# Feed-forward up product of pairs 2 to 21: seven quarter products of 256 columns in place of eight

## The chip, the cores and the metric

The kernel runs on one core of a Trainium2 chip. The metric is the device time of one execution in microseconds (us), lower is better. A core has five engines that matter here: PE (TensorE, the matrix engine, with PEld for its weight loads), DVE (VectorE), ACT (ScalarE), POOL (GpSimd) and SP, which issues most of the DMAs. They run side by side and wait for one another through semaphores.

## The reference, cut to what matters

The reference is two transformer blocks for 512 tokens of width 1024. The change is in the feed-forward part of the first block:

```python
h = _rmsnorm(x, g_pre_ffn[i])                       # 512 tokens x 1024
u = _causal_dwconv(h @ w_up[i], w_conv[i], b_conv[i])  # w_up: 1024 x 5632
a, v = u[..., :D_FF], u[..., D_FF:]                 # D_FF = 2816, 22 tiles of 128
x = x + _rmsnorm((jax.nn.gelu(a) * v) @ w_down[i], g_post_ffn[i])
```

All of it is float32. The product `h @ w_up` is the up product; its first 2816 columns are the gate, the others the value.

## The kernel before, in words

**The precision.** A float32 product is made of three products of rounded parts. Each operand is split into a high part (the value rounded to fp32r) and a low part (the rest), and high x high, high x low and low x high are added up in PSUM. The names ending in `_r` are such fp32r views.

**The tiling.** Weights come from HBM as tiles of 128 x 1024 f32 (512 KB), the list `W`, into the 12 slots of `ring`. The up product has 44 tiles from number `W_UP` on: tile 2j holds the weights of gate features 128j to 128j+127, tile 2j+1 those of the value. A **pair** is such a couple, j = 0 to 21 (`NF` = 22). A tile is eight blocks of 128 x 128, one for each eighth (k) of the width 1024.

**One tile on each engine.** ACT makes the high part (`high_act`, L379: `ring` to `arena_r`, 1024 columns), POOL the low part (`low_pool`, L394: tile minus high), PE runs `split_features`: 16 matmuls of 512 columns with the high weights (L431, tokens high and low in turn) and 8 with the low weights (L434). Split tiles have two places, so the high part of tile t+2 is made when tile t has been used. The tokens are `hT_r` (high) and `up_low`, 128 x 512 for each k.

**Behind the product.** Each tile leaves 128 features x 512 tokens in one of eight PSUM banks. The causal convolution of width 3 along the tokens is three operations: ACT scales and adds the bias from PSUM (`conv_last`, L2763), DVE adds the two shifted taps (L3065 and L3067, scalar_tensor_tensor with `u` in PSUM, the view `banks`, and the sum `c` in SBUF, the view `arena`). When both tiles of a pair are done ACT takes the gelu of the gate (L2770) and DVE multiplies the two (L3071) into `gT`, the rows of the down product that follows.

**The order.** Every engine runs a list written out by hand. PE's list has the 44 tiles one after the other, pair by pair, with one wait on `up_dve` four pairs back. ACT's has, for each tile, the high part of the tile two ahead and then `conv_last`. POOL's has one low part after another. DVE's has four tap operations and one multiplication for each pair. SP loads tile n into its slot when the tile 12 before it has been used. Rows 0 and 1 of the down product's tokens are split by DVE in the last pair, the others behind it, by `split_dve` (L420 the high part, L421 the low).

## Time and profile before

| | before |
|---|---|
| device time, median of 3 runs | 1540.62 us (1538.61 to 1542.84) |
| profiled execution, its own time | 1538.59 us |
| its span (first to last instruction) | 1536.8 us |
| granted TensorE clock, mean | 0.995 |
| PE busy | 1495.9 us, 97% of the span |
| DVE, ACT, POOL busy | 667.6, 508.5, 513.6 us |

The profile is of one execution. Its own time is 1.8 us more than its span and 2.0 us less than the median. An engine's busy time is the union of its instructions; matmuls are pipelined, so the start of one to the start of the next tells what one costs, not its duration. The two letters behind a name tell the direction: `banks<-hT_r,arena_r` writes PSUM from two tensors of SBUF. A name in SBUF is anything but `banks`.

### The profile page before, as it was taken

Reading aid. Unit: us, or ns where it says so; the run is one execution under the profiler, and the core shown is the slowest. Engines: PE = TensorE matmul, PEld = TensorE weight load, DVE = VectorE, ACT = ScalarE, POOL = GpSimd, SP = SyncE. Lnnn points to the kernel's source line nnn. Section 1 sums busy time; section 2 is a strip of 40 time slices with the busy share of each in tenths; the row PEclk is TensorE's granted clock in tenths of the full one; section 3 lists DMA queues with packets and bytes.
Section 4 is the critical chain, followed back from the end, with each engine's and each line's share of the span. In section 5 each row is a group of like instructions: output and inputs, shape, how many; then the busy total and the mean of one; then the engine's idle time right before and its main releaser. Section 6 shows DMA issues by size and latency. Waiting matters only on the chain.

```text
span 1536.8 us, 19531 instructions
## 1 busy us (share of the span) xinstructions
PE 1495.9 (97%) x7629; PEld 1019.5 (66%) x7630; DVE 667.6 (43%) x1141; ACT 508.5 (33%) x917; POOL 513.6 (33%) x328
## 2 busy tenths in 40 slices
PE   8999999999999999999999999999999999999997
PEld 7976677888788888888888777468543443433433
DVE  4157664224733333423335778664533232332334
ACT  4246664223533333321246333424111111111112
POOL 3454664445344444444724362622100010010000
PEclk9999999999999999999999999999999999999999
DMA  8233002322322222232323222267999999999996
GB/s 313 98 109 95 1 2 97 98 100 99 115 96 96 96 96 96 97 97 99 97 92 122 91 82 69 109 256 289 361 429 428 431 418 430 429 429 421 424 426 252
DMA packets 52636, 306.87 MB, mean 200 GB/s; under 512 B 7098, under 2 KB 7354, under 8 KB 40001
## 3 DMA queue, kind: packets, MB, share of 16 engines
q1 hardware_dynamic: 47872, 292.03, 49.2%
q0 software_dynamic: 4096, 11.49, 2.0%
q10 hardware_dynamic: 576, 2.10, 0.3%
q8 instruction: 63, 1.03, 0.3%
q14 instruction: 29, 0.23, 0.1%
HBM read 303.39 MB, written 4.19 MB: 200 GB/s over the span
## 4 chain that ended last, share of the span: by engine, by line
PE 86%; DMA 6%; DVE 5%; ACT 1%; POOL 1%; issue 1%; SPq 0%; DVEq 0%; ACTq 0%
PE banks L431 19%; PE banks L1256 13%; PE banks L476 12%; PE banks L434 9%; DMA ring<-experts 6%; PE banks L1302 5%; PE banks L1311 3%; PE banks L1056 2%; PE banks L456 2%; PE banks L2484 2%; PE banks L2468 2%; PE banks L2550 1%; PE banks L2454 1%; PE banks L914 1%; PE banks L915 1%; PE banks L2443 1%
## 5 line engine op out<-in xcount | busy, mean ns | idle before, releaser
L394 POOL TENSOR_TENSOR arena_r<-ring,arena_r 128x1024 fp32r<-128x1024 f32 x143 | 353.2, 2475 | 414.1 <-ACT arena_r L379 394.5
L379 ACT ACTIVATE arena_r<-ring 128x1024 fp32r<-128x1024 f32 x143 | 150.5, 1058 | 441.4 <-PE banks L434 279.4
L431 PE MATMUL banks<-hT_r,arena_r 128*128 128x512 f32 x640 | 250.0, 391 | 0.0
L431 PE MATMUL banks<-arena_r 128*128 128x512 f32 x640 | 249.1, 389 | 0.0
L1256 PE MATMUL banks<-ring,arena 128*64 128x512 f32 x704 | 222.5, 605 | 12.0 <-DMA ring<-experts 12.0
L476 PE MATMUL banks<-arena_r 128*128 128x512 f32 x784 | 183.5, 389 | 0.6 <-DVE arena_r L421 0.6
L476 PEld LDWEIGHTS banks<-arena_r 128*128 128x128 f32 x784 | 147.1, 188 | 31.5 <-POOL arena_r L394 1.0
L1256 PEld LDWEIGHTS banks<-ring,arena 128*64 128x64 f32 x704 | 70.5, 139 | 142.4 <-issue 141.5
L431 PEld LDWEIGHTS banks<-hT_r,arena_r 128*128 128x128 f32 x640 | 120.1, 188 | 29.0 <-issue 3.4
L431 PEld LDWEIGHTS banks<-arena_r 128*128 128x128 f32 x640 | 120.2, 188 | 25.1 <-issue 0.2
L751 POOL MEMSET arena<- 128x1024 f32 x15 | 14.3, 952 | 341.8 <-PE banks L1209 332.8
L434 PE MATMUL banks<-hT_r,arena_r 128*128 128x512 f32 x520 | 128.4, 389 | 0.0
L1949 DVE TENSOR_TENSOR resid<-resid,banks 128x1024 f32<-128x1024 f32 x60 | 70.6, 1218 | 127.2 <-PE banks L1311 127.2
L1302 PE MATMUL banks<-arena 128*64 128x512 f32 x496 | 113.6, 595 | 2.5 <-DMA arena<-experts 2.2
L1256 PE MATMUL banks<-arena 128*64 128x512 f32 x278 | 115.9, 595 | 0.0
L434 PEld LDWEIGHTS banks<-hT_r,arena_r 128*128 128x128 f32 x520 | 97.6, 188 | 20.3
L3065 DVE SCALAR_TENSOR_TENSOR arena<-banks,colt,arena 128x511 f32<-128x511 f32 x44 | 33.0, 750 | 151.8 <-ACT arena L2763 151.8
L1302 PEld LDWEIGHTS banks<-arena 128*64 128x64 f32 x496 | 36.5, 137 | 66.3 <-issue 60.5
L1311 PE MATMUL banks<-arena_r,colt_r 128*128 128x512 f32 x256 | 67.5, 404 | 0.1
L1518 ACT ACTIVATE arena<-banks 128x512 f32<-128x512 f32 x16 | 9.6, 597 | 165.6 <-PE banks L1268 165.6
L1311 PEld LDWEIGHTS banks<-arena_r,colt_r 128*128 128x128 f32 x256 | 45.5, 188 | 23.4 <-issue 14.6
L1938 DVE SCALAR_TENSOR_TENSOR arena_r<-banks,colt,arena_r 128x512 fp32r<-128x512 f32 x32 | 24.0, 751 | 82.2 <-ACT arena_r L1548 82.2
(506 smaller groups left out, 2171.6 us busy)
## 6 DMA issues: line engine op xcount, KB each, us to landing
ring<-stream SPq DMA_DIRECT2D x164, 512.0 KB, 3.3
arena<-experts SPq DMA_DIRECT2D x35, 2048.0 KB, 15.6
ring<-experts SPq DMA_DIRECT2D x32, 2048.0 KB, 16.6
ring<-experts SPq DMA_DIRECT2D x17, 1024.0 KB, 17.3
arena<-experts SPq DMA_DIRECT2D x31, 512.0 KB, 10.1
arena<-experts SPq DMA_DIRECT2D x11, 1024.0 KB, 15.9
ring<-experts SPq DMA_DIRECT2D x14, 512.0 KB, 6.4
hT<-experts SPq DMA_DIRECT2D x8, 512.0 KB, 11.0
```

What stands on the lines that cost most here:

```text
L379: nc.scalar.activation(parts(name, m)[:, 0, :], tile(tile_n), ACT.Copy).then_inc(S["w_high"], 1)
L394: nc.gpsimd.tensor_tensor(w[:, 1, :], tile(tile_n), plain(w[:, 0, :]), ALU.subtract).then_inc(S["w_low"], 1)
L431: nc.tensor.matmul(pb[:, bank, :], w[:, 0, k * P:(k + 1) * P], b[:, k, :], start=(k == 0 and part == 0), stop=False)
L434: last = nc.tensor.matmul(pb[:, bank, :], w[:, 1, k * P:(k + 1) * P], high[:, k, :], start=False, stop=(k == ND - 1))
L456: last = nc.tensor.matmul(pb[:, bank0 + i, 0:width], a[:, k, i * P:(i + 1) * P], w[:, v, q * width:(q + 1) * width], start=(k == 0 and par ...
L476: last = nc.tensor.matmul(pb[:, 2 * i + h, :], u[row], w[:, v, h * 512:(h + 1) * 512], start=(k == 0 and row + v == 0), stop=(k == K - 1 a ...
L1056: last = nc.tensor.matmul(pb[:, 2 * i + h, :], rows[row][:, i * P:(i + 1) * P], w[:, v, h * 512:(h + 1) * 512], start=(k == 0 and part == ...
L1256: last = nc.tensor.matmul(pb[r, bank, :], XT[:, k, r], weights(b, c + e, k * 512, (k + 1) * 512), start=(k == 0), stop=(k == ND - 1))
L1302: last = nc.tensor.matmul(pb[r, 3 + h, :], hbT[:, k, r], weights(b, 4 + e, at, at + 512), start=(k == 0), stop=(k == 3))
L1311: last = nc.tensor.matmul(pb[:, bank, :], spread_r[:, i * P:(i + 1) * P], y[:, h * 512:(h + 1) * 512], start=(part == 0), stop=(part == 1 ...
L1949: TT(half, half, pb[:, first:second + 1:second - first, :], ALU.add).then_inc(S["added"], 1)
L3065: L(nc.vector.scalar_tensor_tensor(out=c[:, 1:T], in0=u[:, 0:T - 1], scalar=col("w_conv", 2 * NF + m), in1=c[:, 1:T], op0=ALU.mult, op1=AL ...
```

## The change

Pairs 0 and 1 (`PLAIN_PAIRS` = 2) stay as they are. In each of the twenty pairs 2 to 21 (`MIXED`) the two tiles are seen as a 2 x 2 array of quarters: gate or value, by the first or the second half of the width (`gate_1`, `gate_2`, `value_1`, `value_2`, each 128 x 512). The tokens are a 2 x 2 array too: first or second half of the width by the first or last 256 tokens (`x_1` to `x_4`). The product of two 2 x 2 arrays takes eight quarter products; here seven are made (Strassen's scheme in Winograd's form), of sums of weight quarters (`s1` to `s4`) with sums of token quarters (`t1` to `t4`), and the four output quarters are put together from them.

- **PE** runs `up_term` seven times a pair: 8 matmuls of 256 columns with the high part of the term's weights, 4 with the low part.
- **DVE** makes the token sums once (8 operations over 128 x 1024, and four low parts of the same size). For each pair it makes the four weight sums (`weight_sums`, 128 x 512 each) and seven joins (`join`, 128 x 256, a quarter product in PSUM added to something in SBUF), the last of which leave gate and value as rows in `junk`, which is SBUF. The four taps now read `junk` instead of PSUM.
- **ACT** makes seven high parts of 128 x 512 for a pair (`term_high`) in place of two of 128 x 1024, and a copy of the first quarter product (`take_first`).
- **POOL** makes seven low parts of 128 x 512 in place of two of 128 x 1024.
- Each of the seven terms has one place for its split weights, so the high part of term q of pair j+1 waits for PE to be done with term q of pair j. The tiles of these pairs use 6 slots of the ring, the other six hold the parts of `t1`, `t2` and `t4`. Several semaphores are merged under new names (`mg_sig` and `pg_sig` to `gate_sig`, and the like), and the later indices are worked out by `made`.

The diff, cut to its core:

```diff
+TERMS = ["gate_1 x_1", "gate_2 x_2", "s2 t2", "s1 t1", "s3 t3", "s4 x_4", "value_2 t4"]
+PLACES_OF = [(0, 0), (0, 1), (1, 0), (1, 1), (2, 0), (2, 1), (3, 0)]
...
-            low_pool(pool, "up", 2)
+            low_pool(pool, "up", 2, 2 * PLAIN_PAIRS)
+            for j in MIXED:
+                for q in range(NQ):
+                    high, low = term_parts[q][:, 0, :], term_parts[q][:, 1, :]
+                    pool.wait_ge(S["w_high"], term_made(j, q))
+                    nc.gpsimd.tensor_tensor(low, term_source(j, q), plain(high), ALU.subtract).then_inc(S["w_low"], 1)
...
+            def up_term(j, q):
+
+                weight, (high, low) = term_parts[q], t_parts[TERMS[q].split()[1]]
+                pe.wait_ge(S["w_high"], term_made(j, q))
+                for k in range(4):
+                    for part, src in enumerate((high, low)):
+                        nc.tensor.matmul(term_bank(j, q), weight[:, 0, k * P:(k + 1) * P], src[:, k, :], start=(k == 0 and part == 0), stop=False)
+                pe.wait_ge(S["w_low"], term_made(j, q))
+                for k in range(4):
+                    last = nc.tensor.matmul(term_bank(j, q), weight[:, 1, k * P:(k + 1) * P], high[:, k, :], start=False, stop=(k == 3))
+                return last
...
+            for j in MIXED:
...
+                if j > PLAIN_PAIRS + 1:
+                    pe.wait_ge(S["up_sums"], summed(j - 2, "c21"))
+                for q in range(NQ - 1):
...
+                    up_term(j, q).then_inc(S["up_part"], 1)
...
+            def take_first(j):
+                act.wait_ge(S["up_part"], terms_done(j, 1))
+                if j > PLAIN_PAIRS:
+                    act.wait_ge(S["up_sums"], summed(j - 1, "u2"))
+                nc.scalar.activation(first_term, term_bank(j, 0), ACT.Copy).then_inc(S["up_snap"], 1)
...
+            for j in MIXED:
+                if j > PLAIN_PAIRS:
+                    term_high(j, 6)
+                    conv_last(j - 1, 1)
+                take_first(j)
...
+                gelu(j - 1)
...
+                    for q in range(NQ - 1):
+                        term_high(j + 1, q)
+                conv_last(j, 0)
...
+            def weight_sums(j):
+                gate_tile, value_tile = tile(W_UP + 2 * j), tile(W_UP + 2 * j + 1)
+                first, second = slice(0, 512), slice(512, 1024)
...
+                if j > PLAIN_PAIRS:
+                    dve.wait_ge(S["w_low"], term_made(j - 1, 5))
+                nc.vector.tensor_tensor(s_home["s1"], value_tile[:, first], value_tile[:, second], ALU.add).then_inc(summing, 1)
+                dve.wait_ge(summing, summed(j, "s1"))
+                nc.vector.tensor_tensor(s_home["s2"], s_home["s1"], gate_tile[:, first], ALU.subtract).then_inc(summing, 1)
+                nc.vector.tensor_tensor(value_tile[:, first], gate_tile[:, first], value_tile[:, first], ALU.subtract).then_inc(summing, 1)
+                dve.wait_ge(summing, summed(j, "s2"))
+                nc.vector.tensor_tensor(s_home["s4"], gate_tile[:, second], s_home["s2"], ALU.subtract).then_inc(summing, 1)
...
+                u = up_rows[w] if j in MIXED else pb[:, 2 * j + w, :]
...
+                nc.vector.tensor_tensor(to, other, term_bank(j, q), ALU.add).then_inc(summing, 1)
...
+            for j in MIXED:
+                if j > PLAIN_PAIRS:
+                    join(j - 1, "c21")
+                    conv(j - 1, 0)
+                    conv(j - 1, 1)
+                gated_rows(j - 1)
+                join(j, "c11")
+                if j < NF - 1:
+                    weight_sums(j + 1)
...
+                for what in ("u2", "u4", "u3", "c22", "c12"):
+                    join(j, what)
```

What stands in a row on DVE, first before, one pair (`banks` is PSUM, all else SBUF):

```order
408 L3065 SCALAR_TENSOR_TENSOR arena<-banks,colt,arena 128x511
409 L3067 SCALAR_TENSOR_TENSOR arena<-banks,colt,arena 128x510
410 L3065 SCALAR_TENSOR_TENSOR arena<-banks,colt,arena 128x511
411 L3067 SCALAR_TENSOR_TENSOR arena<-banks,colt,arena 128x510
412 L3071 TENSOR_TENSOR arena<-arena 128x512
```

Then DVE now, from one pair's last join to the next pair's (L3244 to L3249 are the weight sums, L3287 the joins, L3261 and L3263 the taps, L3269 the multiplication):

```order
450 L3287 TENSOR_TENSOR junk<-junk,banks 128x256 x3
451 L3261 SCALAR_TENSOR_TENSOR arena<-junk,colt,arena 128x511
452 L3263 SCALAR_TENSOR_TENSOR arena<-junk,colt,arena 128x510
453 L3261 SCALAR_TENSOR_TENSOR arena<-junk,colt,arena 128x511
454 L3263 SCALAR_TENSOR_TENSOR arena<-junk,colt,arena 128x510
455 L3269 TENSOR_TENSOR arena<-arena 128x512
456 L3287 TENSOR_TENSOR junk<-fifth_home,banks 128x256
457 L3244 TENSOR_TENSOR arena<-ring 128x512
458 L3246 TENSOR_TENSOR arena<-arena,ring 128x512
459 L3247 TENSOR_TENSOR ring<-ring 128x512
460 L3249 TENSOR_TENSOR arena<-ring,arena 128x512
461 L3287 TENSOR_TENSOR fifth_home<-fifth_home,banks 128x256
462 L3287 TENSOR_TENSOR junk<-fifth_home,banks 128x256 x2
```

The pair had five operations, one of them with both inputs in SBUF; it has sixteen now, nine of them with both inputs in SBUF (the taps, the multiplication and the sums), and seven joins with one input in PSUM.

POOL before, from the loads in front of the up product to those behind the down product (74 low parts: 42 of the up product and 22 of the down product, with ten others):

```order
76 L2168 DMA grow<-grows 128x1024
77 L394 TENSOR_TENSOR arena_r<-ring,arena_r 128x1024 x74
78 L2177 DMA grow<-grows 128x1024
```

POOL now, at the same place, the first pair of the twenty:

```order
76 L2252 DMA grow<-grows 128x1024
77 L478 TENSOR_TENSOR arena_r<-ring,arena_r 128x1024 x2
78 L2258 TENSOR_TENSOR arena_r<-ring,arena_r 128x512 x2
79 L2258 TENSOR_TENSOR arena_r<-arena,arena_r 128x512 x2
80 L2258 TENSOR_TENSOR arena_r<-ring,arena_r 128x512
81 L2258 TENSOR_TENSOR arena_r<-arena,arena_r 128x512
82 L2258 TENSOR_TENSOR fifth_home_r<-ring,fifth_home_r 128x512
```

Two operations of 1024 columns a pair became seven of 512, each reading two operands in SBUF.

## Rows read from the trace of the kernel before

**Rows 1.** The page: busy us, share of the span, instructions; chain that ended last
```profile
PE 1495.9 (97%) x7629; PEld 1019.5 (66%) x7630; DVE 667.6 (43%) x1141; ACT 508.5 (33%) x917; POOL 513.6 (33%) x328
...
PE 86%; DMA 6%; DVE 5%; ACT 1%; POOL 1%; issue 1%; SPq 0%; DVEq 0%; ACTq 0%
```

**Rows 2.** Chain that ended last, 489 to 512 us: start us, us, what
```profile
499.83 3.63 PE banks L431 x16
...
505.27 3.63 PE banks L431 x16
```

**Rows 3.** Groups, 420 to 640 us: form, count, busy us, mean ns, idle before
```profile
L394 POOL TENSOR_TENSOR arena_r<-ring,arena_r 128x1024 fp32r<-128x1024 f32 x40 | 96.1, 2403 | 128.7 <-ACT arena_r L379 128.7
...
L379 ACT ACTIVATE arena_r<-ring 128x1024 fp32r<-128x1024 f32 x40 | 42.4, 1060 | 136.2 <-PE banks L434 133.5 <-PE banks L447 2.7
L2763 ACT ACTIVATE arena<-banks,colt 128x512 f32<-128x512 f32 x40 | 30.5, 761 | 0.0
L3065 DVE SCALAR_TENSOR_TENSOR arena<-banks,colt,arena 128x511 f32<-128x511 f32 x40 | 30.0, 750 | 139.9 <-ACT arena L2763 139.9
...
L3071 DVE TENSOR_TENSOR arena<-arena 128x512 f32<-128x512 f32 x20 | 15.2, 762 | 1.1 <-ACT arena L2770 0.5
L2770 ACT ACTIVATE arena<-arena 128x512 f32<-128x512 f32 x20 | 12.4, 619 | 0.0
```

**Rows 4.** PE in order of time, 280 columns, first projection: start us, us, instruction
```profile
80.04 0.29 PE L456 MATMUL banks<-arena_r 128*128 128x280 f32 x1
...
80.42 0.29 PE L456 MATMUL banks<-arena_r 128*128 128x280 f32 x1
```

**Rows 5.** PE in order of time, 256 columns, 64 rows, in attention
```profile
176.63 0.28 PE L2454 MATMUL banks<-arena_r,queries_r 64*128 64x256 f32 x2
176.75 0.28 PE L2454 MATMUL banks<-arena_r,grow_r 64*128 64x256 f32 x2
```

**Rows 6.** POOL and DVE in order of time, up product, L3065 reading PSUM
```profile
501.07 2.40 POOL L394 TENSOR_TENSOR arena_r<-ring,arena_r 128x1024 fp32r<-128x1024 f32 x1 [3.03 <-ACT arena_r L379]
...
501.69 0.75 DVE L3065 SCALAR_TENSOR_TENSOR arena<-banks,colt,arena 128x511 f32<-128x511 f32 x1 [3.10 <-ACT arena L2763]
```

**Rows 7.** POOL and DVE in order of time, w_o product, both inputs in SBUF
```profile
377.59 16.45 POOL L394 TENSOR_TENSOR arena_r<-ring,arena_r 128x1024 fp32r<-128x1024 f32 x6 [4.29 <-ACT arena_r L379]
...
378.06 13.72 DVE L421 TENSOR_TENSOR arena_r<-arena,arena_r 128x512 fp32r<-128x512 f32 x5 [2.90 <-ACT arena_r L410]
```

**Rows 8.** POOL alone, in order of time: 1024 columns and 512
```profile
802.63 9.46 POOL L394 TENSOR_TENSOR arena_r<-ring,arena_r 128x1024 fp32r<-128x1024 f32 x4 [8.12 <-ACT arena_r L379]
...
87.74 9.85 POOL L2126 TENSOR_TENSOR hT<-hT_r,arena_r 128x512 f32<-128x512 f32 x8 [4.16 <-PE banks L456]
```

**Rows 9.** POOL and DVE in the first microseconds, in order of time
```profile
28.78 4.99 POOL L394 TENSOR_TENSOR arena_r<-ring,arena_r 128x1024 fp32r<-128x1024 f32 x2 [5.95 <-ACT arena_r L379]
28.93 2.33 DVE L3130 SCALAR_TENSOR_TENSOR arena<-arena 128x64 f32<-128x64 f32 x1
...
31.30 0.23 DVE L3131 SCALAR_TENSOR_TENSOR arena<-arena 128x64 f32<-128x64 f32 x1
```

**Rows 10.** DVE alone, in order of time: both inputs in SBUF, 512 columns
```profile
952.41 0.69 DVE L1634 SCALAR_TENSOR_TENSOR hT<-hT,arena 128x512 f32<-128x512 f32 x1
953.02 0.69 DVE L1635 SCALAR_TENSOR_TENSOR hT<-hT,arena 128x512 f32<-128x512 f32 x1
953.74 0.69 DVE L1636 SCALAR_TENSOR_TENSOR hT<-hT,arena 128x512 f32<-128x512 f32 x1
```

**Rows 11.** Groups of the attention stage, 130 to 235 us: DVE and ACT
```profile
L2970 DVE COPY arena<-banks 128x256 f32<-128x256 f32 x12 | 4.9, 408 | 1.1 <-PE banks L2468 1.1
...
L2712 ACT ACTIVATE arena_r<-arena 128x512 fp32r<-128x512 f32 x4 | 2.3, 633 | 0.0
```

**Rows 12.** DVE behind the last pair, in order of time
```profile
661.02 0.77 DVE L3071 TENSOR_TENSOR arena<-arena 128x512 f32<-128x512 f32 x1
665.86 0.43 DVE L420 CAST arena_r<-arena 128x512 fp32r<-128x512 f32 x1 [4.07 <-PE banks L476]
```

More of the change, by code:

```diff
@@ L2552, in _ @@
                 pe.wait_ge(S["w_low"], at)
-                for w, (high, low, formed_low) in enumerate(branches):
+                for w, (high, low, formed_low, others) in enumerate(branches):
                     for k in range(4):
@@ L2771, in _ @@
+            conv_last(NF - 1, 1)
+            gelu(NF - 1)
             nc.scalar.activation(st[:, 449:450], cs("eps"), ACT.Sqrt)
```

269 lines of the change are left out of this document (208 added, 61 removed).

## The prediction

> **What bounds the kernel now.** I read the page first: PE is busy for 97% of the span and makes 86% of the chain that ended last, while DVE, ACT and POOL are busy for a third of it or little more [rows 1]. Then the chain inside the up product: it is PE alone, and a tile of 24 matmuls begins every 5.44 us (499.83, 505.27) [rows 2]. That is 226.7 ns a matmul of 512 columns and **10.88 us a pair**. Nothing else ends a wait of PE there. Then the groups of that stage [rows 3]: in a pair POOL works 2 x 2.40 us, ACT 2 x 1.06 + 2 x 0.76 + 0.62 = 4.3 us, DVE about 3.8 us (four taps of 0.75 and a multiplication of 0.76). All three are idle most of the time, and what ends their idle time is PE. So PE's time can be taken out one for one, until one of the three, or something two of them share, needs as long as PE.
>
> **PE's part.** Each of the twenty pairs loses 48 matmuls of 512 columns and gets 7 x 12 = 84 of 256. The fp32r matmul nearest to that with all 128 rows has 280 columns: three of them start within 0.38 us, 127 ns each [rows 4]. With 256 columns, on 64 rows and two at a time, the couples follow at 0.12 us [rows 5]. The 24 columns between 280 and 256 are worth 10 ns at the slope of the rows (226.7 - 127 ns for 232 columns), so the bounds are 117 and 127 ns; I take 120. PE then needs 84 x 0.120 = 10.1 us a pair, 0.8 less than now; with the ends 9.8 to 10.7. If PE set the pace, twenty pairs would give 16 us (4 to 21). An eighth of the columns is gone, and part of that is given back in 36 more instructions.
>
> The Trainium skill (TensorE: Matmul & The Clock Gate, Back-to-back issue gap) gives a warm matmul N/2.4 + 2.5 ns apart from its weight load. By that 256 columns are an estimated 109 ns and a pair 9.2 us. The trace's 226.7 ns at 512 columns is 11 ns above the page's 216, so the measured rows are used.
>
> **ACT's part.** Seven high parts of 128x512 at 0.63 [rows 11], the copy of a quarter of 256 columns out of PSUM (nearest row: DVE's 0.41 [rows 11]), two `conv_last` of 0.76 and a gelu of 0.62 [rows 3] make 7.0 us a pair. ACT does not bound.
>
> **POOL's part.** Alone, POOL subtracts 1024 columns every 9.46/4 = 2.37 us and 512 columns every 9.85/8 = 1.23 us [rows 8]. Seven of 512 make 8.6 us a pair, against 4.8 now. That fits under 10.1 us, if nothing stops POOL.
>
> **DVE's part.** An operation with both inputs in SBUF and 512 columns takes 0.61 us to the next, 0.72 when the next waits for its result (952.41, 953.02, 953.74) [rows 10]. A pair has nine of them now: four weight sums, four taps, since these read `junk` and no longer PSUM, and the multiplication. That is 9 x 0.61 = 5.5 us, and about 0.4 more where one waits for the one before. The seven joins of 256 columns read PSUM on one side; nearest row 0.41 [rows 11], 2.7 us. Sum 8.6 us a pair against 3.8. Taken alone this fits too.
>
> **What the two do to each other.** Here the rows speak against the change. In the up product now, POOL and DVE overlap and neither is slower for it: L3065 takes its 0.75 us inside a low part of 2.40 us, because its `u` comes from PSUM [rows 6]. Where a DVE operation has both inputs in SBUF it is otherwise. In the w_o product six low parts of POOL run while DVE makes five subtractions of 128x512. DVE needs 13.72 us for five that alone take 3.0 us (0.61 each [rows 10]), and POOL 16.45 us for six that alone take 14.2 us [rows 7, 8]. They take turns: a DVE operation waits until POOL's is done, and POOL's next one until DVE's is. Each turn costs POOL (16.45 - 14.2)/5 = 0.45 us, so 0.15 us of POOL's operation runs beside DVE's 0.60, and one of 512 columns keeps DVE out for 1.23 - 0.15 = **1.08 us**. Taps are scalar_tensor_tensor, not tensor_tensor; do they take turns as well? With both inputs in SBUF, L3130 over 64 columns took 2.33 us while a low part ran, and the same form 0.23 us beside none (L3131) [rows 9]. They do.
>
> The Trainium skill says the same (SBUF — State Buffer, Who interferes with whom): a DVE instruction with two SBUF inputs contends with a GpSimd instruction that reads SBUF, and the second one to come waits for the whole of the first. By that the change is bound by these turns, and the trace agrees, with 13.72 us for 3.0 us of work.
>
> **The sum.** Per pair there are seven POOL and nine DVE operations that exclude each other. If the shared way never stands idle they take 7 x 1.23 + 9 x 0.60 - 7 x 0.15 = **13.0 us**. That is a floor, and over PE's 10.1. From DVE's side: 8.6 us of its own, plus 1.08 us for each of POOL's operations that gets ahead of one of its own. The five joins in a row (2 us) let one or two of the seven pass without loss. With five in the way it is 14.0 us, with all seven 16.2. I take **13.6 us**, nearer to the floor, since POOL is also held up by ACT and the joins let it catch up. That leaves PE waiting 3.5 us in each pair, for high parts of the sums and for low parts. Twenty pairs: 20 x (13.6 - 10.88) = +54.4 us; at the floor +42, at 16.2 +106.
>
> At the start, DVE makes 12 operations over 1024 columns (about 1.2 us each) and the first weight sums before the third pair's terms can be complete, in the 22 us that pairs 0 and 1 take, with two low parts of POOL in between. ACT's `term_high` of pair 2 stands behind a `gelu` and a `conv_last` that wait for DVE. I allow 3 us of waiting (0 to 8). At the end DVE now finishes its last pair some 8 us behind PE's last matmul, where it was 4; DVE next acts at 665.86, 4 us after its last multiplication at 661.02 [rows 12], and that idle time covers it. I allow 1 us (0 to 4) for the first low part of the down product behind POOL's last term. The loads, the merged semaphores and the new slots cost nothing: six slots hold three pairs, so a tile is asked for two pairs, over 20 us, before it is needed, which covers any landing.
>
> Sum against the profiled execution: 1538.6 + 54.4 + 3 + 1 = 1597. The median of the runs is 2.0 us above that execution, so **1599 us**.
>
> **The rivals.**
> A. *The taps do not take turns.* Only three rows over 64 columns say that they do. Then five DVE operations exclude POOL's: 8.6 + 5 x 0.60 - 0.75 = 10.9 us, and with DVE's own chain about 11.2. That gives 20 x 0.3 + 4 = +10, 1551 us. Against it stands the 2.33 us of [rows 9].
> B. *PE keeps the pace (faster).* The place is POOL's low parts against DVE's sums and taps. If the turns were much cheaper than in [rows 7], so that 8.6 us of POOL and 8.6 us of DVE ran side by side, PE would be last in each pair at 10.1 us, and twenty pairs give 16 us back less 3 at the start: 1528 us. It decides from the point where the seven turns cost POOL less than 10.1 - 8.6 = 1.5 us together, 0.2 us each, where [rows 7] show 0.45 for five and nine come in a pair.
> C. *PE's clock falls.* PE would be idle a quarter of each pair. If its clock went to the lower of its two levels for good, 84 matmuls would take about twice 10.1 us, 20 us a pair: near 1730 us. If only in some stretches, something between. For it speaks only that PE has never been so idle in this stage.
> D. *All seven in the way.* DVE meets POOL's operation each time: 16.2 us, about 1651 us.
>
> **How the numbers follow.** The forecast (turns, 13.0 to 15 us a pair, 1580 to 1632 with the ends of start and end) has 0.80. A has 0.07, B 0.06, C 0.04, D 0.03. The range is 1570 to 1640: the forecast's bounds, opened to 12.5 us a pair below, where a turn overlaps more than I took, and to 15.3 above. It leaves out A, B, C and D, 0.20. Below 1536 only B: faster 0.06. Within 0.3%, about what a measurement of this kernel can tell from no change, 0.03, from between A and B. Slower 0.91.
>
> **What the profile after would show.** Right: about 13.6 us from one pair's first matmul to the next pair's; PE waiting for the ACT and POOL lines of the terms; DVE's sums and taps with durations of 0.7 us in some places and 1.5 to 1.8 in others; POOL's 512-column low parts at a mean well above the 1.23 us of [rows 8]; PE's matmuls of 256 columns 120 ns apart. Wrong: if the taps at L3261 stay at 0.69 us under POOL's work, A holds; if POOL's mean stays there and PE does not wait, B; if the granted clock drops in 440 to 700 us, C. The sum is wrong as well if a pair takes under 13.0 us though the turns are there: then the 1.08 us is too large.

## The result, and the profile after

| | before | after |
|---|---|---|
| device time, median of 3 runs | 1540.62 us (1538.61 to 1542.84) | 1608.62 us (1606.02 to 1608.77) |
| ratio to before | | 1.0436, 95% interval 1.0408 to 1.0464 |
| profiled execution, its own time | 1538.59 us | 1606.02 us |
| its span | 1536.8 us | 1604.2 us |
| granted TensorE clock, mean | 0.995 | 0.979 |

The kernel is 4.4% slower. The page of after, first the busy times, then the chain that ended last, to be held against [rows 1]:

```profile
PE 1514.1 (94%) x8349; PEld 1061.3 (66%) x8350; DVE 872.4 (54%) x1373; ACT 556.4 (35%) x1041; POOL 633.4 (39%) x428
...
PE 66%; DVE 19%; DMA 7%; issue 4%; ACT 2%; POOL 1%; DVEq 0%; SPq 0%; ACTq 0%
```

The chain is the work that ended last, followed back from the end. PE's share of it fell from 86% to 66% and DVE's rose from 5% to 19%, by some 225 us of 1604, and the chain goes through DVE inside the changed stage. What PE itself was doing tells where the 67.4 us between the two spans came in. The starts are those of the first matmul of each piece, read in the PE rows of both traces; pairs 2 to 21 end with PE's last matmul:

| piece | before, us | after, us | difference |
|---|---|---|---|
| start to the up product | 417.94 | 418.16 | +0.2 |
| pairs 0 and 1, and the wait for pair 2 | 21.89 | 26.35 | +4.5 |
| pairs 2 to 21 | 217.60 | 273.55 | +56.0 |
| wait for the first row of the down product | 0 | 6.92 | +6.9 |
| from there to the end | 879.4 | 879.3 | -0.1 |

**One pair.** DVE in order of time (start us, us, engine, line, operation, out<-in, count, idle time before and what ended it), from the weight sums of one pair to those of the next. L3244 to L3249 are the sums, L3287 the joins, L3261 and L3263 the taps, L3269 the multiplication:

```profile
541.25 0.68 DVE L3244 TENSOR_TENSOR arena<-ring 128x512 f32<-128x512 f32 x1
541.97 0.69 DVE L3246 TENSOR_TENSOR arena<-arena,ring 128x512 f32<-128x512 f32 x1
542.58 0.68 DVE L3247 TENSOR_TENSOR ring<-ring 128x512 f32<-128x512 f32 x1
543.18 0.68 DVE L3249 TENSOR_TENSOR arena<-ring,arena 128x512 f32<-128x512 f32 x1
543.78 0.41 DVE L3287 TENSOR_TENSOR fifth_home<-fifth_home,banks 128x256 f32<-128x256 f32 x1
544.29 0.75 DVE L3287 TENSOR_TENSOR junk<-fifth_home,banks 128x256 f32<-128x256 f32 x2
545.15 1.08 DVE L3287 TENSOR_TENSOR junk<-junk,banks 128x256 f32<-128x256 f32 x3
546.78 1.28 DVE L3261 SCALAR_TENSOR_TENSOR arena<-junk,colt,arena 128x511 f32<-128x511 f32 x1 [0.55 <-ACT arena L2876]
548.10 1.66 DVE L3263 SCALAR_TENSOR_TENSOR arena<-junk,colt,arena 128x510 f32<-128x510 f32 x1
549.68 1.78 DVE L3261 SCALAR_TENSOR_TENSOR arena<-junk,colt,arena 128x511 f32<-128x511 f32 x1
551.50 1.66 DVE L3263 SCALAR_TENSOR_TENSOR arena<-junk,colt,arena 128x510 f32<-128x510 f32 x1
553.20 1.66 DVE L3269 TENSOR_TENSOR arena<-arena 128x512 f32<-128x512 f32 x1
554.78 0.41 DVE L3287 TENSOR_TENSOR junk<-fifth_home,banks 128x256 f32<-128x256 f32 x1
555.11 0.68 DVE L3244 TENSOR_TENSOR arena<-ring 128x512 f32<-128x512 f32 x1
```

A pair takes 13.86 us (541.25 to 555.11) and DVE idles only once in it for more than 0.15 us, for 0.55 us. The sums take 0.68 us each and the joins 0.41 or less. The four taps and the multiplication go from 546.78 to 554.78, 8.0 us for work that takes 3.7 us in e3 below, where POOL reads nothing (0.75 us a tap, 0.69 the multiplication). Now POOL in the same microseconds, the seven low parts of one pair:

```profile
543.46 2.80 POOL L2258 TENSOR_TENSOR arena_r<-arena,arena_r 128x512 fp32r<-128x512 f32 x2 [3.01 <-ACT arena_r L2899]
546.23 1.29 POOL L2258 TENSOR_TENSOR arena_r<-ring,arena_r 128x512 fp32r<-128x512 f32 x1
547.48 1.74 POOL L2258 TENSOR_TENSOR arena_r<-arena,arena_r 128x512 fp32r<-128x512 f32 x1
549.17 1.74 POOL L2258 TENSOR_TENSOR fifth_home_r<-ring,fifth_home_r 128x512 fp32r<-128x512 f32 x1
551.02 3.29 POOL L2258 TENSOR_TENSOR arena_r<-ring,arena_r 128x512 fp32r<-128x512 f32 x2
```

Lay the two lists side by side. From 546.23 to 554.31 POOL makes its last five low parts, and each of the four taps and the multiplication ends about 0.55 us after one of them. A low part takes 1.74 us where the lone one takes 1.23 [rows 8], a tap behind the first 1.66 or more where it takes 0.75 in e3. The joins between 543.8 and 546.2 lie inside two low parts and take what they take alone: their second input is in PSUM. The sums are not slowed either, but for another reason. While DVE makes them POOL has nothing to do (3.01 us idle before 543.46), because the next high part on ACT needs one of these sums.

What waited for what between 445 and 715 us: waiting engine and line, what ended the wait, total us, times, longest:

```profile
ACT arena_r L2899 <- DVE arena L3246: 96.3, 19, 5.2
POOL arena_r L2258 <- ACT arena_r L2899: 65.7, 21, 9.3
PE banks L2671 <- ACT arena_r L2899: 39.6, 20, 4.3
```

So it is a ring through DVE. Late sums make late high parts on ACT, those keep POOL and PE waiting, and POOL's low parts then all fall on DVE's taps, which makes the next sums late. PE needs 84 x 120 ns = 10.1 us of the 13.86, so it loses 3.8 us a pair. (Its row shows 1.8 us of that as idle time, since a matmul's shown duration reaches beyond the start of the next.)

**The end of the stage.** The chain of waits of after, in order of time (start us, us, what), is DVE all the way for the last 7 us before the down product (its "issue" pieces, left out here, stand inside the operations):

```profile
717.85 2.85 DVE arena L3263
...
723.37 0.41 DVE junk L3287
723.77 0.35 DVE arena_r L504
...
724.14 0.70 DVE arena_r L505
```

And the PE row there, its idle time in brackets, with a row of POOL and one of DVE in front of it:

```profile
717.81 5.09 POOL L478 TENSOR_TENSOR arena_r<-ring,arena_r 128x1024 fp32r<-128x1024 f32 x2 [0.54 <-ACT arena_r L463]
720.73 2.71 DVE L3269 TENSOR_TENSOR arena<-arena 128x512 f32<-128x512 f32 x1
724.98 5.21 PE L560 MATMUL banks<-arena_r 128*128 128x512 f32 x13 [6.92 <-DVE arena_r L505]
```

PE is done with pair 21 at 718.06 and then waits 6.92 us. DVE is a pair behind: at 717.85 it makes a tap of pair 20, and the split of the down product's first rows stands behind that. The turns are longer there: POOL is already at the first two low parts of the down product, of 1024 columns, and the tap (2.85 us) and the multiplication (2.71 us) beside them take 4.1 us more than their own 0.75 and 0.69.

**The clock.** Busy time of the engines in four stretches of after (us, then PE, PEld, DVE, ACT, POOL with counts, then the granted clock):

```profile
446.00:450.00 4.00, 4.00 (x23) 4.00 (x23) 3.96 (x4) 1.31 (x3) 3.39 (x2) 0.58 0.00 0
453.00:457.00 4.00, 4.00 (x36) 3.98 (x35) 3.01 (x4) 0.83 (x2) 4.00 (x4) 1.00 0.01 2
541.25:555.11 13.86, 12.08 (x92) 11.00 (x90) 12.96 (x17) 6.18 (x11) 10.74 (x7) 1.00 0.31 116
558.20:561.60 3.40, 3.04 (x16) 2.83 (x15) 2.74 (x6) 2.40 (x5) 3.40 (x4) 0.56 0.02 5
```

Where the granted clock is 0.5, the lower level of 1.2 GHz, for most of four microseconds, they hold 23 matmuls of 256 columns, and 36 at the upper level. There are 13 such stretches between 440 and 740 us, eleven of 3.4 us and two of 6.8 (442.5 and 722.4), and PE waits in the pairs of this stage, which it never did in the kernel before (2.28 us, for a high part, just before the one at 558 us). That one has no such stretch there. They cost little, since PE makes up for them out of its idle time: the pair with the 558 us stretch takes 13.85 us like its neighbours. The last one reaches 4 us into the down product.

### The profile page after: what moved, and what is told of

It reads as the page before. It is cut to its first block, busy times and chain, and to the rows that moved or that the text cites. A ratio compares the mean times of both kernels' runs of the same rounds, so it can differ in the third digit from the quotient of the medians.

```text
span 1604.2 us, 21511 instructions
## 1 busy us (share of the span) xinstructions
PE 1514.1 (94%) x8349; PEld 1061.3 (66%) x8350; DVE 872.4 (54%) x1373; ACT 556.4 (35%) x1041; POOL 633.4 (39%) x428
## 4 chain that ended last, share of the span: by engine, by line
PE 66%; DVE 19%; DMA 7%; issue 4%; ACT 2%; POOL 1%; DVEq 0%; SPq 0%; ACTq 0%
PE banks L1340 12%; PE banks L560 12%; PE banks L515 8%; DMA ring<-experts 7%; PE banks L1386 5%; PE banks L518 4%; DVE arena L3263 4%; DVE arena L3261 4%; PE banks L1395 2%; PE banks L540 2%; PE banks L2573 2%; PE banks L1140 2%; PE banks L2557 2%; DVE junk L3287 2%; PE banks L2639 1%
## 5 line engine op out<-in xcount | busy, mean ns | idle before, releaser
L478 POOL TENSOR_TENSOR arena_r<-ring,arena_r 128x1024 fp32r<-128x1024 f32 x103 | 258.5, 2517 | 294.7 <-ACT arena_r L463 275.3
L1340 PE MATMUL banks<-ring,arena 128*64 128x512 f32 x704 | 223.7, 608 | 12.1 <-DMA ring<-experts 11.5
L560 PE MATMUL banks<-arena_r 128*128 128x512 f32 x784 | 185.8, 393 | 7.5 <-DVE arena_r L505 7.5
L560 PEld LDWEIGHTS banks<-arena_r 128*128 128x128 f32 x784 | 148.4, 190 | 39.4 <-issue 7.1
L515 PE MATMUL banks<-hT_r,arena_r 128*128 128x512 f32 x320 | 125.6, 392 | 0.0
L515 PE MATMUL banks<-arena_r 128*128 128x512 f32 x320 | 124.6, 389 | 0.0
L2258 POOL TENSOR_TENSOR arena_r<-arena,arena_r 128x512 fp32r<-128x512 f32 x60 | 90.8, 1525 | 54.6 <-ACT arena_r L2899 54.6
L2258 POOL TENSOR_TENSOR arena_r<-ring,arena_r 128x512 fp32r<-128x512 f32 x60 | 91.9, 1544 | 12.9 <-ACT arena_r L2899 11.1
L2671 PE MATMUL banks<-ring_r,arena_r 128*128 128x256 f32 x320 | 56.2, 329 | 34.3 <-ACT arena_r L2899 34.3
L2671 PE MATMUL banks<-hT_r,arena_r 128*128 128x256 f32 x320 | 82.4, 289 | 5.3 <-ACT arena_r L2899 5.3
L2671 PE MATMUL banks<-arena_r 128*128 128x256 f32 x320 | 81.9, 287 | 0.0
L515 PEld LDWEIGHTS banks<-hT_r,arena_r 128*128 128x128 f32 x320 | 60.1, 188 | 16.6 <-issue 3.4
L515 PEld LDWEIGHTS banks<-arena_r 128*128 128x128 f32 x320 | 60.1, 188 | 12.6 <-issue 0.2
## 6 DMA issues: line engine op xcount, KB each, us to landing
arena<-experts SPq DMA_DIRECT2D x31, 512.0 KB, 10.5
```

The lines of the kernel that those rows point to most:

```text
L478: nc.gpsimd.tensor_tensor(w[:, 1, :], tile(tile_n), plain(w[:, 0, :]), ALU.subtract).then_inc(S["w_low"], 1)
L515: nc.tensor.matmul(pb[:, bank, :], w[:, 0, k * P:(k + 1) * P], b[:, k, :], start=(k == 0 and part == 0), stop=False)
L560: last = nc.tensor.matmul(pb[:, 2 * i + h, :], u[row], w[:, v, h * 512:(h + 1) * 512], start=(k == 0 and row + v == 0), stop=(k == K - 1 a ...
L1340: last = nc.tensor.matmul(pb[r, bank, :], XT[:, k, r], weights(b, c + e, k * 512, (k + 1) * 512), start=(k == 0), stop=(k == ND - 1))
L2258: nc.gpsimd.tensor_tensor(low, term_source(j, q), plain(high), ALU.subtract).then_inc(S["w_low"], 1)
L2671: nc.tensor.matmul(term_bank(j, q), weight[:, 0, k * P:(k + 1) * P], src[:, k, :], start=(k == 0 and part == 0), stop=False)
```

## The experiments

The theory before the first of them: the pair's length is set by DVE and POOL taking turns, through the taps and the multiplication. The rivals: the changed stage is long by DVE's own amount of work, sums above all, or by the length of the ring of waits whatever the turns cost. "The kernel before" beside each run is from the same chip. A period is from one pair's sums to the next pair's, and the wait is PE's in front of the down product.

| run | time, us | before, us | ratio (95%) | period | wait |
|---|---|---|---|---|---|
| after | 1608.62 | 1540.62 | 1.0436 | 13.86 | 6.9 |
| e1 rows for the taps in PSUM | 1559.86 | 1537.97 | 1.0142 (1.0125 to 1.0158) | 11.33 | 4.4 |
| e2 gelu in PSUM too | 1555.09 | 1537.97 | 1.0106 (1.0089 to 1.0122) | 10.89 | 4.0 |
| e3 memset for the low parts | 1532.53, one run | 1537.97 | | 10.08 | 0 |
| e4 one input for the low parts | 1562.48, one run | 1538.99 | | 11.33 | 1.7 |
| e5 no weight sums | 1557.61, one run | 1537.97 | | 11.02 | 2.4 |
| e6 split of rows 0, 1 earlier | 1610.01 | 1538.99 | 1.0462 (1.0441 to 1.0483) | 13.9 | 7.7 |
| e7 e2 with sums from PSUM | 1537.53 | 1538.99 | 0.9996 (0.9980 to 1.0012) | 10.08 | 0 |
| e8 e7, two high parts earlier | 1538.29 | 1538.99 | 1.0000 (0.9991 to 1.0010) | 10.08 | 0 |
| e9 e8, copies later | 1535.27 | 1538.47 | 0.9977 (0.9965 to 0.9989) | 10.08 | 0 |
| e10 e7, copies later | 1533.80 | 1538.47 | 0.9965 (0.9952 to 0.9977) | 10.08 | 0 |

### e1: the taps read PSUM

```diff
-                u = up_rows[w] if j in MIXED else pb[:, 2 * j + w, :]
+                u = up_row(j, w) if j in MIXED else pb[:, 2 * j + w, :]
...
-                q, other, to = {"c11": (1, first_term, gate_row[:, 0:256]), ...
+                q, other, to = {"c11": (1, first_term, gate_out[:, 0:256]), ...
```

The last join of each quarter writes its sum into a PSUM bank of the pair (`gate_out`, `value_out`), and the taps and `conv_last` read it there. PE's wait two pairs back becomes one on the taps, since these are now the last to read the bank. DVE does the same operations in the same order.

> The same arithmetic as the changed kernel, but the last joins write gate and value into PSUM banks 0 and 1 of the pair, so the four taps of a pair read PSUM and have one input in SBUF, as in the kernel before. DVE has the same number of operations, and the taps alone take 0.75 us instead of 0.69. Theory (turns between POOL and DVE operations with both inputs in SBUF, 1.08 us of POOL in DVE's way each): five such DVE operations a pair are left instead of nine, a pair takes 11.2 us (10.9 to 11.6) instead of 13.85, PE waits about 1 us a pair, the kernel takes 1552 us (1545 to 1562). Rival (DVE is slow by its own length and by the waits between its dependent operations, not by POOL): 13.9 us a pair, about 1608 us.

The period fell from 13.86 to 11.33 us, and the ratio to the kernel before from 1.044 to 1.014, both inside what was expected. The groups of e1 between 480 and 640 us (count, busy us, mean ns, idle before):

```profile
L3250 DVE TENSOR_TENSOR arena<-arena,ring 128x512 f32<-128x512 f32 x14 | 23.3, 1667 | 0.5
L3267 DVE SCALAR_TENSOR_TENSOR arena<-banks,colt,arena 128x510 f32<-128x510 f32 x30 | 22.5, 748 | 1.1
...
L3248 DVE TENSOR_TENSOR arena<-ring 128x512 f32<-128x512 f32 x14 | 20.3, 1448 | 0.0
```

The taps are at 748 ns as in [rows 3], against means of 1.53 and 1.66 us of the two forms in after, between 480 and 640 us. The turns did not all go away: the low parts that used to fall on the taps now fall on the first two sums (1448 and 1667 ns against 0.68 us). The place of the taps' input is the larger part of the loss, and DVE's amount of work, which is the same, is not.

### e2: the multiplication reads PSUM too

```diff
-  nc.scalar.activation(ga[:, j % 2, :], cva[:, j % 2, 0, :], ACT.Gelu_apprx_tanh).then_inc(S["up_gelu"], 1)
+  nc.scalar.activation(up_row(j, 0) if j in MIXED else ga[:, j % 2, :], cva[:, j % 2, 0, :], ACT.Gelu_apprx_tanh).then_inc(S["up_gelu"], 1)
```

> As e1_taps_psum, and the gelu of the gate goes to PSUM too, so the multiplication has one input in SBUF; four DVE operations a pair (the weight sums) are left with both inputs there. Theory of turns: 7 x 1.23 + 4 x 0.60 - 0.6 = 10.4 us at the floor, 10.7 us a pair expected, so PE is nearly the bound; 1541 us (1534 to 1550). Rival (DVE's own length): 13.9 us a pair, 1608 us.

The multiplication fell to 691 ns and the period to 10.89 us. Of the sums, one is still at 1667 ns and the other at 1126, where it was 1448. That leaves the pair 0.8 us over PE's. The period was near the expected 10.7 us, but the time, 1555 us, missed the expected 1541 (1534 to 1550). The pieces of its trace, against the kernel before, say where the rest lies: the up product is entered 4.1 us later, pairs 0 and 1 with the wait take 4.5 us more, pairs 2 to 21 2.6 more, the wait for the down product is 4.0, and what follows takes 2.3 more.

### e3: low parts without a read

```diff
-  nc.gpsimd.tensor_tensor(low, term_source(j, q), plain(high), ALU.subtract).then_inc(S["w_low"], 1)
+  nc.gpsimd.memset(plain(low), 0.0).then_inc(S["w_low"], 1)
```

> The changed kernel with the low parts of the mixed pairs' weights set to zero by a memset of 128x512 on POOL in place of the subtraction (the precision of these products is left out; PE does all its matmuls). POOL then reads nothing in SBUF in this stage, DVE does all its work with nine operations that have both inputs in SBUF. Theory of turns: no turn is left, DVE's own 8.6 us fit under PE, a pair takes PE's 84 x 0.120 = 10.1 us, 1535 us (1528 to 1543), taps and multiplication at 0.69 us. Rival (DVE's own length or the chain through joins, convolution and gelu): a pair stays above 13 us.

Two groups of e3, 480 to 640 us, and PE in 20 us of that stretch:

```profile
L2258 POOL MEMSET arena_r<- 128x512 f32 x96 | 50.3, 526 | 78.1 <-ACT arena_r L2899 78.1
L3263 DVE SCALAR_TENSOR_TENSOR arena<-junk,colt,arena 128x510 f32<-128x510 f32 x32 | 24.0, 750 | 1.1
```

```profile
541.25:561.25 20.00, 20.00 (x169) 20.00 (x168) 17.40 (x33) 12.59 (x22) 7.35 (x14) 1.00 0.29 100
```

Every DVE operation is at its own length (sums 684 to 692 ns, taps 750, multiplication 692), whether a memset runs beside it or not (16 of 16 multiplications and 30 of 63 taps in this stretch have one beside them). PE does not wait from pair 2 on, and the period is 84 x 120 ns = 10.08 us. DVE makes all that it makes in after. So its own work, and the ring of waits with it, fit under PE. Both rivals fall. The memset is shorter than the subtraction as well (0.53 us against 1.23), so this run does not tell POOL's length from POOL's reading; e7 does.

### e4: low parts that read one operand

```diff
-  nc.gpsimd.tensor_tensor(low, term_source(j, q), plain(high), ALU.subtract).then_inc(S["w_low"], 1)
+  nc.gpsimd.tensor_scalar(low, plain(high), 0.0, None, ALU.mult).then_inc(S["w_low"], 1)
```

> The changed kernel with the low parts of the mixed pairs' weights made by one tensor_scalar of 128x512 on POOL (high part times zero; the precision of these products is left out): POOL reads one input in SBUF, for about 0.7 us, where e3_memset_low read none for 0.53 us. Theory (what excludes a DVE operation with both inputs in SBUF is any POOL operation that reads SBUF): taps and sums are stretched again, to a mean of 0.9 us or more, against 0.69 to 0.75 in e3, and a pair takes 10.1 to 11 us. Rival (only POOL operations with two inputs exclude them): durations as in e3 and 10.08 us a pair.

This one missed on a size, and on the pair (11.33 us where 10.1 to 11 were expected). The operation took a mean of 1676 ns in most of its places and no less than 1.48 us anywhere, longer than the subtraction with two inputs:

```profile
L2258 POOL TENSOR_SCALAR arena_r<-arena_r 128x512 fp32r<-128x512 f32 x85 | 140.4, 1676 | 0.0
L3261 DVE SCALAR_TENSOR_TENSOR arena<-junk,colt,arena 128x511 f32<-128x511 f32 x28 | 29.3, 1045 | 7.7 <-ACT arena L2876 7.7
```

POOL had no idle time, and seven of its operations, 1.62 us from start to start, are the period. It does say one thing: a low part with one input holds a DVE operation with two up as well, so the rival falls, but by some 0.3 to 0.4 us and not by 0.8 or more. The first tap of each row takes 1045 ns against 748 in e3, the multiplication 981 against 692, two of the sums 992 and 1098 against 684; the second tap (750) and the other two sums are at their own length though POOL is busy beside them.

### e5: no weight sums

The four DVE sums are left out, and ACT and POOL take the plain quarters in their place.

```diff
-SUMS = ["s1", "s2", "s3", "s4"]
+SUMS = []
...
-                nc.vector.tensor_tensor(s_home["s1"], value_tile[:, first], value_tile[:, second], ALU.add).then_inc(summing, 1)
...
```

> The changed kernel without the four weight sums of a pair: the terms take quarters of the tiles as they are (the sums are left out of the computation). Five DVE operations with both inputs in SBUF are left, taps among them, and the high parts no longer wait for sums. Theory of turns: 10.9 us a pair (10.6 to 11.6), 1546 us. If it were the wait of the high parts for the sums that sets the pace and not the turns, PE would keep it at 10.1 us a pair, 1530 us, and POOL's low parts would still be stretched.

The period is 11.02 us, with the taps and the multiplication still stretched (1367, 1668 and 1670 ns). POOL is busy for 20.00 of 20 us. It is now POOL that makes the pair: seven low parts of 1.23 us and five turns at 0.45 us each are 10.9 us. With the sums the pair takes 2.8 us more, near their own length (2.53 us from 541.25 to 543.78 in after). That fits sums that cost what they take and not a turn; it does not show it, since another engine sets the pace here.

### e6: the split of the down product's first rows earlier

```diff
                     conv(j - 1, 0)
+                    if j == NF - 1:
...
+                        split_dve(dve, chain, "down", gT, 0, 2)
                     conv(j - 1, 1)
```

> The changed kernel, with DVE's split of rows 0 and 1 of the down product moved ahead, between the two convolutions of pair 20 instead of behind them and the multiplication. Theory (PE's 6.9 us of waiting at the start of the down product is DVE being behind with what stands ahead of the split in its list): PE starts the down product about 4.5 us earlier after its last quarter product, waiting 2 to 3 us, and the kernel takes 1604 us instead of 1608.6. Rival (the first weights of the down product, made by ACT and POOL, are as late): PE waits 6 us or more all the same.

The theory failed. The wait did not shrink: it is 7.67 us, and something else ends it. The time, 1610 us, is that of after within the intervals (1.0462 and 1.0436 of the kernel before). PE's row, and four of DVE's in front of it:

```profile
717.89 1.52 DVE L504 CAST arena_r<-arena 128x512 fp32r<-128x512 f32 x1
...
720.05 2.57 DVE L504 CAST arena_r<-arena 128x512 fp32r<-128x512 f32 x1
722.65 2.71 DVE L505 TENSOR_TENSOR arena_r<-arena,arena_r 128x512 fp32r<-128x512 f32 x1
...
726.84 0.69 DVE L3269 TENSOR_TENSOR arena<-arena 128x512 f32<-128x512 f32 x1
```

```profile
727.59 4.80 PE L560 MATMUL banks<-arena_r 128*128 128x512 f32 x11 [7.67 <-DVE arena L3269]
```

In its list PE waits for two things there, the split rows and the multiplication of pair 20 (`up_g` at 21), and the second now stands behind the first on DVE. My theory took the split for what PE lacked; what it lacked was all of DVE's list up to there. The runs in which DVE keeps up (e3, e7 to e10) have no wait at all at that place.

### e7: the sums read PSUM as well

On top of e2, ACT copies one quarter of each tile of the next pair into two PSUM banks that are free (`copies`), and three of the four sums take one input from there.

```diff
...
+                nc.scalar.activation(copy_place(j, 0), tile(W_UP + 2 * j + 1)[:, 512:1024], ACT.Copy).then_inc(S["up_snap"], 1)
+                nc.scalar.activation(copy_place(j, 1), tile(W_UP + 2 * j)[:, 0:512], ACT.Copy).then_inc(S["up_snap"], 1)
...
+                    value_2, gate_1 = copy_place(j, 0), copy_place(j, 1)
```

> As e2_gelu_psum, and from pair 3 on ACT copies value_2 and gate_1 of the next pair into two PSUM banks that are free then, so three of the four weight sums read one input in PSUM; only s4 has both in SBUF. Same result as the changed kernel. Theory of turns: 7 x 1.23 + 0.60 - 0.15 = 9.1 us of turns, DVE's own 9.5 us, ACT 8.3 us, all under PE's 10.1; a pair takes 10.1 to 10.3 us instead of e2's 10.89, PE runs into the down product without a wait, and the kernel takes 1534 us (1529 to 1540), level with the kernel before or a little under it. Rival (e2's 10.89 is set by something else than turns, such as ACT or the sums' chain): no change or slower with ACT's two copies, 10.9 us a pair or more, 1555 us.

Groups of e7 between 480 and 640 us:

```profile
L2276 POOL TENSOR_TENSOR arena_r<-ring,arena_r 128x512 fp32r<-128x512 f32 x50 | 64.2, 1297 | 10.8 <-ACT arena_r L2917 10.8
...
L3297 DVE SCALAR_TENSOR_TENSOR arena<-banks,colt,arena 128x510 f32<-128x510 f32 x32 | 24.0, 749 | 1.1
...
L3283 DVE TENSOR_TENSOR arena<-ring,arena 128x512 f32<-128x512 f32 x16 | 12.2, 764 | 0.0
```

POOL makes the same subtractions as in after, a mean of 1.30 us for these against 1.55, DVE the same sixteen operations, ACT two more. One DVE operation of a pair has both inputs in SBUF where nine had. The period is 10.08 us and PE does not wait from pair 3 on. This is the run that settles the cause: no work was taken away from POOL or DVE, only the place of what DVE reads (and of what some joins and the gelu write) moved from SBUF to PSUM. It is level with the kernel before, though, and not 16 us faster. PE waits 4.3 us in front of pair 2, and pair 2 takes 16.66 us: ACT's copies for pair 3 wait for the last tap of pair 1 and hold four high parts behind them, so PE waits 3.5 us before the fourth term.

### e8, e9, e10: the start of the stage

e8 moves two high parts of pair 2 ahead of the first gelu in ACT's list. e10 is e7 with `copies(3)` moved behind the high parts of terms 3 to 6 of pair 2 (the fourth to the seventh) and the gelu; e9 has both moves. The cut below is the move of `copies`.

```diff
                 take_first(j)
-                if j == PLAIN_PAIRS:
-                    copies(j + 1)
                 if j == PLAIN_PAIRS:
                     for q in (3, 4, 5, 6):
                         term_high(j, q)
                 gelu(j - 1)
+                if j == PLAIN_PAIRS:
+                    copies(j + 1)
```

> As e7_act_copies, with ACT's first two high parts of pair 2 moved ahead of gelu(0), which waits for DVE. Theory (the first mixed pair starts late because of that wait): PE's first matmul of 256 columns follows the last of 512 within 0.5 us instead of about 1, and pair 2 takes 11 us instead of 12.2; 2 us less than e7. If DVE's token sums set the start instead, POOL's two earlier low parts get in DVE's way there and pair 2 stays at 12 us or more: no difference.

In e8 pair 2 began 4.5 us earlier within the stage (21.9 us after the first matmul of pair 0, against 26.4 in e7) and then took 21.22 us. What it gained, it waited for again, and the time did not move. The ACT row that says why:

```profile
452.24 0.60 ACT L2924 ACTIVATE banks<-ring 128x512 f32<-128x512 f32 x1 [4.37 <-DVE arena L3297]
```

ACT stood for 4.37 us at the copies, which need the last tap of pair 1, with the high parts of four terms behind them. That tap ends no earlier than in e7, about 34 us after the stage's first matmul in both. And PE waits a second time, 4.7 us before the third term, which e7 does not have; e9 shows that one alone.

> The kernel with ACT's copies and the early high parts, with one more move in ACT's list: the high parts of terms 3 to 6 of pair 2 and the gelu of pair 1 now stand ahead of ACT's two copies for pair 3. In the version before, those copies waited for the last tap of pair 1 (4.37 us of ACT's idle time) and held the four high parts behind them, so that PE's fourth term of pair 2 began at 454.05 and pair 2 took 21.2 us. Theory (this wait is what the gain was lost to): the high parts come at 448 to 450, POOL's low parts end at about 454, pair 2 takes about 15 to 16 us, pair 3 begins at about 455 in place of 461, and the stage ends 5 to 6 us earlier, 1533 us (0.996 to 0.997 of the kernel before). Rival (DVE's weight sums for pair 3, which stand behind the taps, the multiplication and the copies, set the start of pair 3): pair 2's terms end earlier, but pair 3's third term waits, and under 2.5 us of it is left, 1536 us or more.

> The same move of ACT's copies alone, without the early high parts. Pair 2 then begins at 446.05 as in the kernel with ACT's copies. Theory: pair 2 takes 10.5 to 11.5 us in place of 16.66, pair 3 begins at about 457, the stage ends about 5 us earlier, 1533 us. Rival (the weight sums for pair 3 come too late for its third term): 2 us or less, 1536 us. If this one and the one with the early high parts end within 1 us of each other, the early start of pair 2 is worth nothing by itself, since what follows is set by DVE's list.

Both moved the time: e10 is 0.35% faster than the kernel before, e9 0.23%. In both, pair 3 begins at 460.0 us, 38.3 and 38.5 us after the stage's first matmul, whether pair 2 begins at 443.56 (e9, 16.44 us for the pair) or at 447.86 (e10, 12.15 us). The stages end within 0.2 us of each other, so the early start is worth nothing by itself, as the expectation of e10 said for that case; its reason, that DVE's list sets what follows, does not hold for pair 3. In neither run does PE wait at pair 3 or in it, so DVE's sums for pair 3, the rival of both, are not what kept it.

In e9 PE waits inside pair 2, before the third term. Its high part stands in ACT's list behind the gelu of pair 0, which waits for DVE, and DVE is held up by the very low parts that were moved forward: two of DVE's own operations on the token sums (L3288, 1024 columns, both inputs in SBUF) take 4.58 us together, against 2.35 in e10. First e9's rows, then e10's:

```profile
442.36 4.58 DVE L3288 TENSOR_TENSOR ring_r<-x_sums,ring_r 128x1024 fp32r<-128x1024 f32 x2
451.31 2.05 PE L2689 MATMUL banks<-ring_r,arena_r 128*128 128x256 f32 x8 [4.67 <-ACT arena_r L2917]
...
442.16 2.35 DVE L3288 TENSOR_TENSOR ring_r<-x_sums,ring_r 128x1024 fp32r<-128x1024 f32 x2
```

That is what e8's expectation named as its second case.

For e10 the expected 5 us came out as 4.5 us of shorter stage (230.0 us from the first matmul of pair 0 to the down product, 234.5 in e7), and as 0.9965 of the kernel before in place of 0.9996. Its pair 2 was expected at 10.5 to 11.5 us and took 12.15, 2.1 more than 84 x 120 ns. Of that 1.3 us are in the first term, which runs at the lower clock behind PE's wait of 4.34 us (its twelve matmuls go from 447.86 to 450.59, and the granted clock is 0.50 there), and 0.5 us are a wait of the fourth term for a low part of POOL.

```profile
447.86 0.58 PE L2689 MATMUL banks<-hT_r,arena_r 128*128 128x256 f32 x1 [4.34 <-ACT arena_r L2917]
...
450.59 0.40 PE L2689 MATMUL banks<-hT_r,arena_r 128*128 128x256 f32 x1
...
455.04 0.74 PE L2692 MATMUL banks<-ring_r,arena_r 128*128 128x256 f32 x4 [0.35 <-POOL arena_r L2276]
```

e9's stage is as short (229.8), its time 1.5 us longer than e10's and between its two expectations. In the two traces the difference, 1.9 us of span, lies behind the stage: from the down product's first matmul to the end e9 takes 882.4 us and e10 880.4, and e9 has 23 us of lower clock there, e10 15. One trace each does not tell whether that belongs to the version.

Where e10's 4.8 us of span come from, by the same pieces as in the first section: the up product is entered 3.6 us later; pairs 0 and 1 with the wait take 4.5 us more; pairs 2 to 21 take 203.7 us, 13.9 less; the rest takes 1.1 more. The 3.6 us lie far ahead of the changed code, where the granted clock of e10 is 0.90 between 113 and 130 us and that of the traced execution before is 1.00. It is 1.00 in the traces of after and of e8 too, which have the changed code and enter the up product at 418.2 and 418.1 us, so the 3.6 us do not come with the change as such. The mean clock of the 16 runs of the kernel before beside it goes from 0.991 to 0.995, that of e10's seven from 0.990 to 0.994. What makes an execution fall to the lower clock there stays open.

## Why the prediction was right, point by point

**The forecast case held**: the median is 1608.62 where 1599 was predicted, inside the range, and by the mechanism named. Against the profiled execution the sum was 9 us short (1597 against 1606.02), and the terms below say where.

- **What bounds the kernel before.** Right. With DVE and POOL out of one another's way (e3, e7) PE's time did come out of the stage, 0.8 us a pair, as the reading of [rows 2, 3] said.
- **PE, 120 ns a matmul.** Right: the median from start to start is 120 ns, and e3, e7 and e10 have periods of 84 x 120 ns = 10.08 us. That the figure lay between the 117 and 127 ns of [rows 4, 5] was enough.
- **ACT and POOL alone.** ACT was busy for 6.2 us of a pair (7.0 predicted), POOL 10.7 with its turns. (Seven joins at 0.41 are 2.9 us and not the 2.7 of DVE's sum; in e3 DVE is busy 8.8 us a pair where 8.6 were predicted.) Neither bounds in after; POOL does in e5.
- **Taps take turns, rival A.** The reading from rows over 64 columns [rows 9] held: taps take 1.28 to 1.78 us in the pair shown, 0.75 in e3. Their own length was taken as 0.69, from operations of another form [rows 10]. e1 is A made true by hand, and has about A's period of 11.2 us (11.33).
- **The pair, 13.6 us.** The twenty pairs average 13.68 us, and DVE's period settles at 13.86. That the guess, taken between two sums, came within 0.1 us of the average is partly luck: the first pairs were shorter, and the settled pair is nearer to the upper sum. Of the two sums that framed the guess, DVE's own with five low parts in the way, 14.0 us, fits what happened: exactly five of seven fall on taps and multiplication. The joins let the other two pass, as said. The sums were counted among the turns, and in after they are not, because POOL is out of work while they are made. The settled period stays off the floor of 13.0 us for that reason: the shared way does stand idle. By PE's starts single pairs took from 12.1 to 15.2 us, so the sign "under 13.0 us" had to be read on DVE's period or the average and not on one pair.
- **The start, 3 us.** It was 4.5. ACT's two high parts of pair 2 do stand behind the gelu that waits for DVE, which was named; DVE's own `x_low` operations and weight sums, ahead of that tap in its list, make it late. In e5, without the four sums (2.5 us), the start costs 1.9 us.
- **The end, 1 us.** Wrong: 6.9 us. The step that failed is "that idle time covers it". It looked at rows behind the last pair, where DVE has time. But PE's first need is rows 0 and 1, which DVE splits before it takes up the last pair, and DVE reaches them late, since it works a pair behind PE when it sets the pace; 4.1 us of turns with the down product's low parts of 1024 columns come on top. The term had to be DVE's lag when PE runs out of terms. This term is 5.9 of the 9 us that the sum was short; the pairs are 1.6 (56.0 against 54.4) and the start 1.5. The loads cost nothing, as said: between 445 and 715 us no wait is ended by a DMA.
- **The clock, rival C.** It was given as all or nothing or "something between". It came in stretches, most of 3.4 us, which cost next to nothing while DVE set the pace. By the prediction's own sign (the granted clock drops in 440 to 700 us) C would hold, though its time does not: the sign did not tell stretches from a lasting fall.
- **Rivals B and D.** B did not happen, but its point of decision is what e7 reaches: the pair is PE's as soon as the turns are gone. D was not reached, since two of seven low parts meet only joins and sums.

## What to carry to other kernels

Before moving work to an idle engine, count for each DVE operation how many inputs it reads from SBUF, and lay POOL's operations beside them in time: fewer multiplications bought with operations of two SBUF inputs beside a busy POOL cost 68 us here, and the same operations, eight of the nine with one input in PSUM, gave a gain of 5 us once ACT's list was put in order too. An engine that sets the pace is also late at the end of its stage, so the wait at the next stage's first instruction is its lag and has to be priced from its list, not from its idle time further on. And work moved ahead in one engine's hand-written list can hold up another engine's list, and then nothing is gained (e8, and e9 against e10).

## What the runs showed of the hardware that I had not expected

- **A cast with one SBUF input is held up by POOL as well.** In e6 L504 takes 1.52 us beside a low part of 512 columns and 2.57 beside one of 1024, 0.41 us beside none (at 723.70 in after). The Trainium skill (SBUF — State Buffer, Who interferes with whom) lists casts among the operations that can enter a mode which takes the port shared with GpSimd; these two rows agree. The same section says that a GpSimd instruction that only writes SBUF does not contend with a DVE instruction of two SBUF inputs, and e3's memsets agree, with taps at 750 ns.
- **A one-input POOL operation was slower than the two-input one**: 1.48 us or more for tensor_scalar over 512 columns of fp32r in e4, 1.23 us for the subtraction [rows 8]. It held DVE's operations up for 0.3 to 0.4 us only, as shown under e4.
- **The granted clock falls to the lower level in short stretches** in after, where PE loses 3.8 us a pair to waits: 13 times between 440 and 740 us, mostly for 3.4 us, and it is back at the upper level while PE works on.
